# The first eight modulation groups of a two-block kernel, moved from the vector engine to column strips of the tensor engine

## What is computed

```python
def first_block(x, c, positions, w_in, ..., w_ada, b_ada, g_mix, g_ffn, ...):
    c_act = jax.nn.silu(c)
    for layer in range(DEPTH):
        mod = c_act @ w_ada[layer] + b_ada[layer]
        sh1, sc1, gt1, sh2, sc2, gt2 = jnp.split(mod[:, None, :], N_MOD, axis=-1)
        h = rmsnorm(x, g_mix[layer]) * (1 + sc1) + sh1
        x = x + (1 + gt1) * mixer(h, positions, w_in[layer], ...)
```

## Time and profile before

| | us |
|---|---|
| time, three runs | 2701.70, 2699.28, 2699.52 (median 2699.52) |
| the profiled execution | 2699.71 |
| its span | 2697.9 |
| TensorE busy | 2617.3 (97%) |
| VectorE busy | 1937.0 (72%) |
| ScalarE busy | 1224.2 (45%) |
| mean DMA rate | 207 GB/s |

### The profile page before, as it was taken

How to read it: one execution, slowest core, us unless ns; L and a number is a source line. 1 busy time by engine, 2 the same in 40 slices (tenths; PEclk the granted TensorE clock), 3 DMA queues, 4 the chain that set the end, 5 groups by cost and what they waited for, 6 DMA issues and landing times.

```text
span 2697.9 us, 39482 instructions
## 1 busy us (share of the span) xinstructions
PE 2617.3 (97%) x14741; PEld 2283.7 (85%) x14741; DVE 1937.0 (72%) x2749; ACT 1224.2 (45%) x1595; POOL 101.7 (4%) x145
## 2 busy tenths in 40 slices
PE   5799999999998999999999999998999999999998
PEld 4788888888887888888888888887888888888887
DVE  6987778886888888855666657998676644566554
ACT  2245644444554655544555552004454443444443
POOL 0011111100001000000000000000000000000000
PEclk7699999999999999999999999999999999999999
DMA  9898677765777777755666554552666555666554
GB/s 361 306 299 258 214 249 241 246 202 161 230 255 237 234 246 248 239 186 188 189 190 188 187 164 145 152 154 83 204 181 190 187 188 190 189 190 187 188 187 133
DMA packets 492727, 557.35 MB, mean 207 GB/s; under 512 B 18872, under 2 KB 458425, under 8 KB 492345
## 3 DMA queue, kind: packets, MB, share of 16 engines
q1 hardware_dynamic: 474169, 488.50, 56.4%
q0 software_dynamic: 18432, 67.12, 8.0%
HBM read 553.45 MB, written 2.10 MB: 206 GB/s over the span
## 4 chain that ended last, share of the span: by engine, by line
PE 91%; DVE 5%; DMA 3%; issue 1%; ACT 1%; SPq 0%; POOL 0%; DVEq 0%; ACTq 0%
PE ps L1631 53%; PE ps L1633 26%; PE ps L1961 8%; DMA att<-in_w_ada 2%; DVE wlo L949 1%; DVE tCDE L1072 1%; PE ms L1979 1%; PE ms L1682 0%; DVE att L1072 0%; PE ms L1815 0%; PE ms L1662 0%; DVE norm_rows L1053 0%; PE ms L1705 0%; DVE norm_rows L988 0%; DMA ada<-in_w_ada 0%
## 5 line engine op out<-in xcount | busy, mean ns | idle before, releaser
L949 DVE TENSOR_TENSOR wlo<-raw,whi 128x1024 fp32r<-128x1024 f32 x794 | 971.1, 1224 | 612.8 <-ACT whi L582 603.8
L1631 PE MATMUL ps<-xhl,whi 128*128 128x512 f32 x4352 | 1385.9, 400 | 15.5 <-DVE xhl L1529 6.4
L582 ACT CAST whi<-raw 128x1024 fp32r<-128x1024 f32 x794 | 831.7, 1051 | 1059.7 <-PE ps L1633 1049.2
L1633 PEld LDWEIGHTS ps<-xhl,wlo 128*128 128x128 f32 x4352 | 822.9, 189 | 195.3
L1633 PE MATMUL ps<-xhl,wlo 128*128 128x256 f32 x4352 | 859.5, 279 | 0.0
L1631 PEld LDWEIGHTS ps<-xhl,whi 128*128 128x128 f32 x4352 | 669.1, 190 | 25.6 <-issue 25.3
L1631 PE MATMUL ps<-ghl,whi 128*128 128x512 f32 x1024 | 319.5, 393 | 0.0
L1633 PEld LDWEIGHTS ps<-ghl,wlo 128*128 128x128 f32 x1024 | 192.2, 188 | 44.5
L1961 PE MATMUL ps<-xg,raw 128*128 128x256 f32 x1024 | 221.3, 379 | 0.0
L1631 PE MATMUL ps<-fhl,whi 128*128 128x512 f32 x704 | 219.3, 392 | 0.0
L1961 PEld LDWEIGHTS ps<-xg,raw 128*128 128x128 f32 x1024 | 194.5, 190 | 26.4
(11 more groups left out here) (263 smaller groups left out, 1452.2 us busy)
## 6 DMA issues: line engine op xcount, KB each, us to landing
raw<-in_w_in SPq DMA_DIRECT2D x176, 512.0 KB, 4.4
raw<-in_w_up SPq DMA_DIRECT2D x176, 512.0 KB, 3.9
ada<-in_w_ada POOLq DMA_DIRECT2D x128, 512.0 KB, 4.8
raw<-in_ffn_w_up SPq DMA_DIRECT2D x128, 512.0 KB, 3.8
raw<-in_ffn_w_down SPq DMA_DIRECT2D x128, 512.0 KB, 3.4
raw<-in_conv_w_pw SPq DMA_DIRECT2D x96, 512.0 KB, 3.7
raw<-in_w_down SPq DMA_DIRECT2D x88, 512.0 KB, 3.3
att<-in_w_ada SPq DMA_DIRECT2D x32, 1024.0 KB, 8.7
```

The costliest lines, as they stand in the source:

```text
L582: nc.scalar.copy(whi[t % SPL][:, :, :], raw[t % RAW][:, :, :]).then_inc(s_hi, 1)
L949: nc.vector.tensor_tensor(wlo[t % SPL][:, :, :], raw[t % RAW][:, :, :], whi[t % SPL][:, :, :].bitcast(F32), ALU.subtract).then_inc(s_lo, 1)
L1631: mm(o[:, m, :, :], whi[t % SPL][:, c, m * P:(m + 1) * P], x, start=first and c == 0, stop=last and c == KC - 1, skip_group_check=True)
L1633: ins = mm(o[:, m, 0, :], wlo[t % SPL][:, c, m * P:(m + 1) * P], x[:, 0, :], start=False, stop=last and c == KC - 1, skip_group_check=True)
```

## The change

The vector engine's products of the first eight groups go, and all 16 chunks of a group are multiplied on TensorE, with the weights now as the moving operand:

- ScalarE makes `cact_strips`: each value of `cact` repeated over 32 columns (one activation of 128 x 512).
- `first_piece(n, q)` is one quarter, now called a piece: four float32 products, chunk j with its 32 stationary columns, 512 moving columns, and its output in partitions 32j to 32j+31 of a PSUM bank: one column strip of the array each. The four pieces of a group add up in the same bank. There are 32 pieces, 128 products.
- After a group's fourth piece ScalarE copies the bank to SBUF (`rows_copied`), and `first_columns(n)` sums the four strips and turns the row to columns by 4 products of 128 x 1 with `one_of_strip`, which is 1 in one partition of each strip.
- The five buffers are one ring: piece i waits until TensorE has multiplied piece i-5 (before: until VectorE had used the same quarter of the group before).
- x is fetched ahead of all pieces, and the first two `raw` pieces after group 1 instead of 2.
- The norm's squares are added up by VectorE (`add_older`, 6 additions of 128 x 512), and TensorE sums only two of them over partitions (4 products instead of 16).
- Units 0, 1 stand among the pieces of group 2, units 2, 3 among those of group 4, unit 4 behind the last piece, then the last `first_columns`, then units 5 to 7. `first_columns(n)` stands behind piece 0 of group n+1.
- In `norm_first` scaling and splitting alternate from chunk to chunk. GpSimd's first fetches wait for piece 30. The rounds of the square sums are renumbered by one in the rest of the program, which the diff here leaves out.

```diff
@@ -46,8 +46,8 @@
-BY_TENSOR = 2
-BY_VECTOR = DC - BY_TENSOR
+FIRST_RING = 5
+STRIP = 32
...
@@ -229,7 +218,8 @@
-        first_sum = [[ch(26, 28), ch(28, 30)], [tCDE[:, 0:NCOL], tCDE[:, NCOL:2 * NCOL]]]
+        first_rows = [ch(26, 28), tCDE[:, 0:NCOL]]
+        cact_strips = tCDE[:, NCOL:2 * NCOL].rearrange("p (c s) -> p c s", c=DC)
...
@@ -425,7 +414,9 @@
-        first_bank = (bank_m, bank_z, bank_f)
+        def row_bank(n):
+
+            return ps[n][:, 0, :, :].rearrange("p a t -> p (a t)") if n < 2 else (bank_z, bank_f)[n % 2]
...
@@ -440,18 +431,13 @@
-            def first_quarter(n, q):
-
+            def first_piece(n, q):
+
+                i = 4 * n + q
+                if i >= FIRST_RING:
+                    sp.wait_ge(s_firstmm, i - FIRST_RING + 1)
                 cols_at = slice(FIRST[n] * NCOL, (FIRST[n] + 1) * NCOL)
-                if q == 0:
-                    if n >= 2:
-                        sp.wait_ge(s_firstmm, n - 1)
-                        sp.wait_ge(s_first, products_by(n - 2, 0))
-                    sp.dma_start(ada_q0[n % 2][:, :, :], w_ada[0][:, :, cols_at]).then_inc(s_adaq0[n % 2], 16)
-                else:
-                    if n:
-                        sp.wait_ge(s_first, products_by(n - 1, q))
-                    sp.dma_start(ada_first[q][:, :, :], w_ada[q][:, :, cols_at]).then_inc(s_adaring[q], 16)
+                sp.dma_start(ada_first[i % FIRST_RING][:, :, :], w_ada[q][:, :, cols_at]).then_inc(s_adaring[i % FIRST_RING], 16)
...
@@ -482,20 +468,20 @@
             w_in = blocks("w_in")
-            for q in (1, 2, 3):
-                first_quarter(0, q)
             x_in = A["x"].rearrange("b (c p) (h t) -> p (b c) h t", p=P, t=T)
             for c in range(2):
                 sp.dma_start(att[:, 8 * c:8 * c + 8, :], x_in[:, c]).then_inc(s_in[2], 16)
-            first_quarter(0, 0)
+            for q in range(4):
+                first_piece(0, q)
+            first_piece(1, 0)
             sp.dma_start(posi, A["positions"]).then_inc(s_in[1], 16)
             load_vectors(sp, other_vecs, s_vin[1])
             sp.dma_start(cons[:, C_SW128:], A["consts"][:, C_SW128:]).then_inc(s_rest, 16)
             for n in range(1, ADA_START):
-                for q in range(4):
-                    first_quarter(n, q)
-                if n in (2, 3, 5, 6):
-                    quad = {2: 0, 3: 1, 5: 2, 6: 3}[n]
+                for q in range(1 if n == 1 else 0, 4):
+                    first_piece(n, q)
+                if n in (1, 3, 5, 6):
+                    quad = {1: 0, 3: 1, 5: 2, 6: 3}[n]
                     for k in range(2):
                         load(0, 2 * quad + k, w_in[quad][:, :, CW * k:CW * (k + 1)])
...
@@ -542,13 +528,17 @@
+            nc.gpsimd.memset(one_of_strip[:, :], 0.0).then_inc(s_const, 1)
+            pool.wait_ge(s_const, 4)
+            for j in range(4):
+                nc.gpsimd.memset(one_of_strip[STRIP * j:STRIP * j + 1, :], 1.0).then_inc(s_const, 1)
...
                 if m < 2:
-                    pool.wait_ge(s_first, BY_VECTOR * (ADA_START - 1))
+                    pool.wait_ge(s_firstmm, 4 * ADA_START - 2)
...
@@ -622,17 +612,27 @@
             act.wait_ge(s_trc, 1)
-            nc.scalar.activation(cact[:, :], cols[:, AT["c"]:AT["c"] + DC], ACT.Silu).then_inc(s_cact, 1)
+            c_cols = cols[:, AT["c"]:AT["c"] + DC]
+            nc.scalar.activation(cact_strips[:, :, :], c_cols.unsqueeze(2).to_broadcast([P, DC, STRIP]), ACT.Silu).then_inc(s_cact, 1)
+            nc.scalar.activation(cact[:, :], c_cols, ACT.Silu).then_inc(s_cact, 1)
             for b in range(DC // 2):
                 act.wait_ge(s_tr, b + 2)
                 nc.scalar.copy(res[:, 2 * b:2 * b + 2, :].rearrange("p c t -> p (c t)"), (bank_z, bank_f)[(b + 1) % 2]).then_inc(s_trx, 1)
+            for i in range(DC // 2):
+                act.wait_ge(s_trx, i + 1)
+                new_square(0, i)
+
+            def rows_copied(n):
+
+                act.wait_ge(s_firstmm, 4 * n + 4)
+                nc.scalar.copy(first_rows[n % 2], row_bank(n)).then_inc(s_rows, 1)
+
+            rows_copied(0)
             for b in range(2):
                 act.wait_ge(s_tr, 9 + b + 1)
                 lo = P + 4 * P * b
                 nc.scalar.copy(cols[:, lo:lo + 4 * P], (bank_z, bank_f)[(9 + b) % 2]).then_inc(s_trc, 1)
-            for i in range(DC // 2):
-                act.wait_ge(s_trx, i + 1)
-                square(i, i)
+            root(0)
 
             def first_hi(j):
 
@@ -640,14 +640,17 @@
                     act.wait_ge(s_nt, c + 1)
                     nc.scalar.activation(xh[:, c, :], sq[:, c % 4, :], ACT.Identity, bias=mod[:, c:c + 1]).then_inc(s_nh, 1)
 
-            root(0)
+            rows_copied(1)
             first_hi(0)
             for j in range(1, 4):
-                for t in range(2 * (j - 1), 2 * j):
-                    split_hi(0, t)
+                if j < 3:
+                    split_hi(0, 2 * j - 2)
+                    split_hi(0, 2 * j - 1)
+                rows_copied(2 * j)
                 if j == 3:
-                    split_hi(0, 6)
-                    split_hi(0, 7)
+                    for t in range(4, 8):
+                        split_hi(0, t)
+                rows_copied(2 * j + 1)
                 first_hi(j)
...
@@ -1053,33 +1056,12 @@
-            def first_products(n, beside):
...
@@ -1105,43 +1087,35 @@
+                def scaled(c):
+                    nc.vector.scalar_tensor_tensor(sq[:, c % 4, :], res[:, c, :], gmod[:, 0, c:c + 1], rstd[:, :], ALU.mult, ALU.mult).then_inc(s_nt, 1)
+                scaled(c0)
                 for c in range(c0, c0 + 4):
-                    nc.vector.scalar_tensor_tensor(sq[:, c % 4, :], res[:, c, :], gmod[:, 0, c:c + 1], rstd[:, :], ALU.mult, ALU.mult).then_inc(s_nt, 1)
-                for c in range(c0, c0 + 4):
+                    if c + 1 < c0 + 4:
+                        scaled(c + 1)
                     dve.wait_ge(s_nt, c + 1)
                     dve.wait_ge(s_nh, c + 1)
                     nc.vector.scalar_tensor_tensor(xl[:, c, :], sq[:, c % 4, :], mod[:, c:c + 1], xh[:, c, :].bitcast(F32),
                                                    ALU.add, ALU.subtract).then_inc(s_h, 1)
...
+            for j in range(1, 7):
+                add_older(0, j)
+            dve.wait_ge(s_in[1], 16)
+            nc.vector.tensor_copy(posf, posi).then_inc(s_posf, 1)
+            read_first(0)
+            root(0, EPS1, s_var2, 1)
+            for j in range(4):
+                if j:
+                    read_first(2 * j)
+                if j == 3:
                     for t in range(4, EARLY):
                         split_lo(0, t)
-
-            dve.wait_ge(s_cact, 1)
-            for n in range(ADA_START):
-                first_products(n, beside)
-            read_first(ADA_START - 2)
-            read_first(ADA_START - 1)
-            norm_first(3)
+                read_first(2 * j + 1)
+                norm_first(j)
+                if j < 2:
+                    split_lo(0, 2 * j)
+                    split_lo(0, 2 * j + 1)
+            dve.wait_ge(s_cact, 2)
             dve.sem_inc(s_chain, DC * (1 + ADA_START))
...
@@ -1683,26 +1657,23 @@
+            def first_piece(n, q):
+
+                i = 4 * n + q
+                pe.wait_ge(s_adaring[i % FIRST_RING], 16 * (i // FIRST_RING + 1))
+                for j in range(4):
+                    ins = mm(row_bank(n)[STRIP * j:STRIP * (j + 1), :], cact_strips[:, 4 * q + j, :], ada_first[i % FIRST_RING][:, j, :],
+                             start=q == 0, stop=q == 3, skip_group_check=True)
+                ins.then_inc(s_firstmm, 1)
+
             def first_columns(n):
 
...
+                a = 4 * FIRST[n]
+                pe.wait_ge(s_rows, n + 1)
+                if n:
+                    pe.wait_ge(s_firstmod, n)
+                for m in range(4):
+                    ins = mm(bank_m[:, a + m:a + m + 1], first_rows[n % 2][:, P * m:P * (m + 1)], one_of_strip[:, 0:1], start=True, stop=True)
                 ins.then_inc(s_gemv, 1)
@@ -1724,35 +1693,46 @@
-            first_columns(0)
+            pe.wait_ge(s_cact, 1)
+            pe.wait_ge(s_const, 8)
+            for q in range(4):
+                first_piece(0, q)
+            first_piece(1, 0)
             pe.wait_ge(s_vin[1], 16 * len(other_vecs))
             for b in range(2):
                 pe.wait_ge(s_trx, 7 + b)
                 turned(9 + b, [att[:, 17 + 4 * b + i, 0:P] for i in range(4)])
-            first_modulation(0)
-            statistic(0)
+            first_columns(0)
             pe.wait_ge(s_posf, 1)
             mm(bank_o[:, T:2 * T], ones[0:1, :], posf, start=True, stop=True).then_inc(s_posb, 1)
+            older_sum(0)
+            newest_sum(0)
+            for q in range(1, 4):
+                first_piece(1, q)
             pe.wait_ge(s_trc, 3)
-            first_columns(1)
-            first_modulation(1)
...
```

(17 more changed lines are left out.)

137 lines of the change are left out of this document (34 added, 103 removed).

## The result

The changed kernel is slower: 2711.15 us (median) against 2701.09 us for the kernel before on the same chip, ratio 1.0037, 95% interval 1.0027 to 1.0047. The forecast was 2687.5 us and faster. The profiled executions took 2697.9 us of span before and 2709.5 after, a difference of 11.6 us.

The account below looks back on a forecast made before the run. Entry bound by DMA, less 7 us VectorE holds it back, plus a long tail; main loop by TensorE. 137.3 - 123.1 - 2.2 = 12.0 us off 2699.5 gives 2687.5; likeliest 2681 to 2694, 8-in-10 range 2681 to 2730.

Parts of the forecast that it names:

- The transfers: Entry: 41.1 MB up to the last piece at 405 GB/s, last landing at 108 us (105 to 111).
- DMA just doesn't starve.: Entry: a TensorE stand of 4 us plus two units, 10 us, fits the 13 us held by five buffers.
- rival D: Entry: ring too short, 14 us stand with cold units against 13, twice; 3 to 5 us lost, 2691; within the 0.60.
- A piece on TensorE: Entry: four products of a piece take 1.73 us, halves of neighbouring strips running in pairs.
- rival C: Entry: all four strips run at once, 0.86 us a piece; 2687 to 2690, within the forecast's 0.60.
- Rival A: Entry: strips don't overlap in float32, 3.46 us a piece, TensorE becomes the bound; 2727 us, chance 0.18.
- The 163 ns for a change between strips and whole array: Entry: array may run empty at some 24 changes, nearly all in slack; 0.2 us on the path.
- Rival B: Entry: strips overlap but clock stays at 0.50 for much of it; 2744 if always low, chance 0.07 in full.
- The tail: Entry's end: last landing to last sums at 113.6 us, then 9.5 us to the first group, hence 123.1.
- The restart of the clock: Units at the entry's end: one restart at low clock charged, 2.2 us.
- The main loop: After the entry: as long as before, 2560.6 us; no term contains a longer one.
- rival B's mild form: Entry: clock low for a third of the time, 2.3 us a piece; 2694 to 2712 us, chance 0.13.

Follow-up runs that it names:

- the kernel with later units: Changed kernel with one_of_strip moved behind small, and units 0 to 3 one group later (beside groups 3 and 5): 2688.49 us, ratio 0.9953.
- the kernel without the 32 bytes: Changed kernel with one_of_strip placed behind small, so every other tensor keeps its address from the kernel before: 2695.74 us, ratio 0.9981.

## Why the forecast was wrong

The forecast was 2687.5 us, the measurement 2711.15: 23.6 more. Half of it lies in the entry, which ended at 137.06 us where 123.1 + 2.2 = 125.3 was forecast (11.8), and half in the main loop, 2709.5 - 137.06 = 2572.4 us for 2560.6 (11.8).

**The transfers** (forecast: last landing 108 us; 13.9 later). The size was right: 109.2 us once two things are taken away that the forecast had not, at the 405 GB/s it used. The address of the targets costs 121.9 - 116.0 = 5.9 us, which no step of it knew. The ring costs 116.0 - 109.2 = 6.8.

**"DMA just doesn't starve."** This is the step that failed in the entry. It set a stand of 4 us and two units, 10 us, against 13 us of buffers. The stand was right, 4.28 us. But the unit behind it runs at clock 0.50 (5.4 us for it, 53.66 to 59.05, and not 2.8): in the rows above, a piece starts at 47.46, and the one behind the first unit at 59.05, the one behind the second at 63.10. That is 13.7 us from the end of the first in which only one buffer comes free, the 14 us that rival D had worked out (from two cold units; the second ran at full clock, and pieces took the rest). And 14 against 13 doesn't yet give 6.8 us lost. The 13 us counted five empty buffers, but when the stand began at 49.4 us one of the five was full, with the piece that had landed at 49.1. The other four landed by 59.8; the next could be issued only at 60.3 and landed at 65.2, the one behind it at 72.2 (in the kernel with later units, which had issued them by 56.4, these two landed at 65.4 and 67.9). So four buffers, 10.4 us, stood against 13.7, twice. I had the case and priced it inside the forecast, at 2691, as if it were a variant; and the earlier trace rows already showed clock 0.50 where TensorE had had little to do.

**A piece on TensorE** (forecast 1.73 us, by halves that go in pairs). Measured 0.93 at full clock: rival C. Nothing hung on it, since TensorE was not the bound. Rival A is out for this kernel, since its pieces overlap. The run with one strip measured 2727.25 where A's sum said 2727, and its pieces cost what A had said (3.50 for 3.46), but that the totals agree so closely is luck: the 27 pieces started at 38.4 us and not at 31, and the 8 us of stands that A had counted aren't in that run, where the units stand a group later. The Trainium skill ("TensorE: Matmul & The Clock Gate", Part 3) gives 2.38 times for three strips; four float32 strips made 3.8 here. The 163 ns for a change between strips and whole array were not measured by themselves; behind the last piece they can't be more than about 0.1 us, since unit 4 starts at 122.91, 1.00 us after that piece, and pieces in a row take 0.93.

**Rival B** (the clock stays low) is out only in its price. Its sign came true, as the stretch from 30 to 108 us of the changed kernel shows (columns as in the earlier trace rows):

```profile
30.00:108.00 78.00, 56.38 (x295) 29.42 (x294) 19.93 (x42) 14.40 (x25) 0.00 (x0) 0.72 0.96 346
```

A mean clock of 0.72 is the low level in over half of the time. But a piece took 1.93 us at 0.50 and not 3.46, still less than the 2.7 us of its transfer, so the pieces didn't hold the entry up. The low clock cost time through the unit behind each stand, and so through the ring. In the kernel with later units the same stretch has 0.78, and no dip.

**The tail** (forecast 5.6 us from the last landing to the sums, then 9.5). Measured 4.9 us, from 121.9 to 126.8, and 10.3, in the changed kernel; 5.0 and 10.3 in the one with later units (109.2, 114.2, 124.50). The last group is read out by VectorE, and TensorE waits 1.8 us for it in both. In sum this term was 0.1 off (15.2 for 15.1).

**The restart of the clock** (one, 2.2 us). Right in kind and a little too dear: the changed kernel has one, right behind 137.88 us and so in the main loop's account, for 1.7 us; the kernel with later units has none there and pairs of products of 0.63 us from the start.

**The main loop** (2560.6 us, "which no term here contains"). Of its 11.8 us more, 1.7 are the restart just named. From there to the last split it was 9.2 us longer: 7.7 by the place of `att_r`, `fhl` and `ghl` against the weights, 1.4 by the clock near 870 us. The last 0.9 lie behind the last split, and I have no cause for them. This is the other step that failed, and with the 5.9 us of the transfers, which have the same origin, the larger one. The forecast took the main loop's instructions as unchanged, and they were. The place of their operands was not, and it could be read in the diff: one line that adds a tensor ahead of `att`.

Put together: 2688.49 us is what the change gives without either, and the forecast was 2687.5. The ring adds 7.2 us (2695.74) and the 32 bytes 15.4 (2711.15: 5.9 by the transfers, 7.7 by the operands, and the 1.7 of the restart, which the kernel without the 32 bytes doesn't have). The idea and its sum were right; the measured kernel also contained a tensor in a bad place and a ring that was too short. That 2711.15 lies in the range of 2681 to 2730 is no merit of the cases: the range reached that far for rival A, which did not happen, and rival B's mild form (2694 to 2712) holds the number by pieces slower than their transfers, which there were not.

## What to carry to other kernels

Where an edit adds or resizes a tensor, compare the addresses of all others first: give the targets of large transfers a multiple of 256 bytes, and keep the moving operand off the places past the weight buffers that were slow here (160 and 224 bytes, modulo 256); then try the place 64 bytes past those buffers, which was worth 15 to 17 us here. Judge a change with its new tensors placed where they move nothing, or a small idea is measured together with a larger accident. And a ring has to cover the stand of its consumer plus the cold work behind it, not the stand alone, and only with the buffers that are not yet full when the stand begins.

## What the runs showed of the hardware

- The place of the moving float32 operand against the weights changes a product's time at full clock: a unit (8 products with `whi`, 8 with `wlo`) took 2.760 to 2.826 us. Moving all tensors together changes nothing in it; the place of `whi` against `wlo` counts too (2.800 where `wlo` stood 64 bytes further off). The mechanism is open.
- Transfers with runs of 2 KB moved 409 GB/s into targets at a multiple of 256 bytes and 387 into any other tried (32, 64 and 128 bytes off).
- Four float32 products with 32 stationary and 512 moving columns took 0.93 us in four strips and 3.50 in one, both at full clock: 3.8 times.
- Together these give 2671.38 us, 1.1% under the kernel before, of which the change itself brings 0.5% with its new tensor out of the way and its units a group later. Not tried: `raw`, the target of the main loop's transfers, at a multiple of 256 bytes; it starts 128 bytes past one here, and 160 and 192 in the two kernels with all tensors shifted.
